# A hybrid decoder trunk on one core: the first projection in another order, index scores and two blocks' search rounds two units earlier

## What is computed

```python
h = rmsnorm(x, norm_mix[l])
proj = h @ w_in[l]
(u, dq, dk, dv, iq, ik, iw, rq, rk, rv, rg) = jnp.split(proj, split_pts, axis=-1)
y_a = s5_mixer(u, ...)                       # state space model on u, 256 wide
y_b = dsa_attention(dq, dk, dv, iq, ik, iw, rel_bias)
y_c = retention(rq, rk, rv, rg, ret_gn[l])
x = x + jnp.concatenate([y_a, y_b, y_c], -1) @ w_out[l]
x = x + swiglu(rmsnorm(x, norm_ffn[l]))

# inside dsa_attention, for a block of 128 queries
dots  = einsum('bqhd,bsd->bqhs', iq, ik)                       # 4 index heads
score = einsum('bqhs,bqh->bqs', relu(dots), iw)
_, sel = top_k(where(causal, score, NEG_INF), 256)             # 256 keys are kept
# softmax attention (8 heads, one shared key and value head) over the kept keys
```

## Time and profile before

| | us |
|---|---|
| median of 3 runs | 2590.75 |
| lowest, highest | 2588.12, 2592.52 |
| the profiled execution | 2596.5 |
| its span, first to last instruction | 2594.7 |
| TensorE busy | 2515.0 (97%) |
| VectorE, ScalarE, GpSimd busy | 1370.1 (53%), 1136.5 (44%), 1319.2 (51%) |
| mean granted clock of TensorE | 0.988 |

### The profile page before, as it was taken

One profiled execution on the slowest core, in us unless ns is written; L12 is line 12 of the kernel. 1 busy time (PEld: TensorE's weight loads), 2 busy tenths in 40 slices (PEclk: granted clock), 3 DMA queues, 4 the chain that ended last, 5 costly groups with the idle time before them and its releaser, 6 DMA issues.

```text
span 2594.7 us, 34756 instructions
## 1 busy us (share of the span) xinstructions
PE 2515.0 (97%) x13515; PEld 1997.8 (77%) x13515; DVE 1370.1 (53%) x2559; ACT 1136.5 (44%) x1726; POOL 1319.2 (51%) x818
## 2 busy tenths in 40 slices
PE   8998979999999999999999999999999999999998
PEld 6777657778777877788777887777887788888887
DVE  3788766987852226842421395589786322211112
ACT  5242355676545433324344422466755453322222
POOL 3432245464645654545555632554655457565654
PEclk9998999999999999999999999999999999999999
DMA  6241112232222353223322342222222225233332
GB/s 169 83 150 42 50 50 90 61 94 74 76 69 66 99 163 98 81 82 90 90 76 81 88 135 58 81 66 82 78 78 63 68 66 203 77 107 101 102 117 89
DMA packets 385666, 232.92 MB, mean 90 GB/s; under 512 B 29592, under 2 KB 371552, under 8 KB 383072
## 3 DMA queue, kind: packets, MB, share of 16 engines
q1 hardware_dynamic: 385136, 229.62, 29.8%
q10 hardware_dynamic: 368, 1.08, 0.1%
HBM read 213.88 MB, written 14.69 MB: 88 GB/s over the span
## 4 chain that ended last, share of the span: by engine, by line
PE 83%; DVE 12%; ACT 2%; issue 2%; DMA 0%; POOL 0%; DVEq 0%; ACTq 0%; SPq 0%
PE psum L1873 79%; PE psum L2203 2%; DVE scores L1431 2%; DVE top L1429 2%; DVE scores L1413 1%; DVE search_i L1453 1%; DVE xs L1245 0%; PE psum L2232 0%; ACT xs L1118 0%; PE psum L2028 0%; DVE scratch L1538 0%; DVE h_lo L1310 0%; PE psum L2307 0%; DVE tmp L1306 0%; ACT xs L1100 0%
## 5 line engine op out<-in xcount | busy, mean ns | idle before, releaser
L769 POOL TENSOR_TENSOR w_lo<-w_raw,w_hi 128x1024 fp32r<-128x1024 f32 (+2 forms) x408 | 902.8, 2213 | 1132.5 <-ACT w_hi L883 1132.4
L1873 PE MATMUL psum<-h_hi,w_hi 128*128 128x512 f32 x1984 | 796.7, 402 | 21.3 <-DVE tmp L1385 8.2
L883 ACT ACTIVATE w_hi<-w_raw 128x1024 fp32r<-128x1024 f32 (+2 forms) x408 | 397.5, 974 | 899.5 <-PE psum L1873 855.6
L1873 PE MATMUL psum<-h_lo,w_hi 128*128 128x512 f32 x1984 | 765.3, 393 | 0.9 <-POOL h_lo L777 0.9
L1873 PE MATMUL psum<-h_hi,w_lo 128*128 128x512 f32 x1984 | 515.7, 391 | 0.0
L1873 PEld LDWEIGHTS psum<-h_hi,w_hi 128*128 128x128 f32 x1984 | 375.4, 189 | 134.7 <-issue 43.9
L1873 PEld LDWEIGHTS psum<-h_lo,w_hi 128*128 128x128 f32 x1984 | 375.0, 189 | 79.0 <-issue 2.2
L1873 PEld LDWEIGHTS psum<-h_hi,w_lo 128*128 128x128 f32 x1984 | 374.1, 189 | 76.9
L1245 DVE TENSOR_TENSOR xs<-xs,psum 128x512 f32<-128x512 f32 x160 | 110.0, 688 | 330.5 <-PE psum L1873 319.6
L1873 PE MATMUL psum<-a_hi,w_hi 128*128 128x512 f32 x704 | 279.3, 397 | 1.1 <-DVE xs L1245 1.1
L1873 PE MATMUL psum<-a_lo,w_hi 128*128 128x512 f32 x704 | 274.6, 390 | 0.0
(11 more groups left out here) (333 smaller groups left out, 3066.1 us busy)
## 6 DMA issues: line engine op xcount, KB each, us to landing
w_raw<-in_w_ffn_in_dram SPq DMA_DIRECT2D x176, 512.0 KB, 3.8
w_raw<-in_w_ffn_out_dram SPq DMA_DIRECT2D x96, 384.0 KB, 3.1
w_raw<-in_w_in_dram SPq DMA_DIRECT2D x68, 512.0 KB, 3.8
w_raw<-in_w_out_dram SPq DMA_DIRECT2D x32, 512.0 KB, 3.6
x_half<-xs SPq DMA_DIRECT2D x8, 1024.0 KB, 6.1
xs<-x_half SPq DMA_DIRECT2D x8, 1024.0 KB, 6.8
w_raw<-in_w_ffn_out_dram SPq DMA_DIRECT2D x32, 256.0 KB, 2.7
out_dram<-mixed SPq DMA_DIRECT2D x8, 512.0 KB, 4.3
```

The costliest lines, as they stand in the source:

```text
L769: eng.tensor_tensor(w_lo(u, n), w_raw[:, u % 3, 0:n], w_hi[:, u % 2, 0:n].bitcast(F32), ALU.subtract).then_inc(sems["weights_ready"], 1)
L883: act(w_hi[:, u % 2, 0:n], w_raw[:, u % 3, 0:n], ACTF.Copy).then_inc(sems["hi_ready"], 1)
L1873: return eng.matmul(out_, lhsT, rhs, start=start, stop=stop, skip_group_check=True)
```

## The change

The first projection of layer 0, half 0, makes its first six units in another order: values and keys, the index key, the two index queries, and then the two S5 inputs. `made` gives the content of a place, `unit_at` the place of a content; the other three projections are as they were. The weight loads, the evictions, the doubling transfers of `kT` and `ikT`, the transposes of `gate` and the waits for `iqT` follow.

With that, steps move. The first `scores` step stands behind unit 4 (it stood behind unit 6), the last behind unit 8 (10). Of the S5 parameters, step 2 stays behind unit 6, step 3 moves from unit 10 to 7 and step 4 from unit 11 to 9. Block 2's 16 rounds all lie in the first projection (10 did). In the second projection block 3's rounds start behind unit 1 of it (unit 4), and 17 of them (12) are in front of the attention steps, which are blended with the 15 (20) that are left.

```diff
+INDEX_FIRST = (U_VK, U_II, U_IQ, U_IQ + 1, 0, 1)
+def made(l, h, i):
+    return INDEX_FIRST[i] if (l, h) == (0, 0) and i < U_RET else i
+def unit_at(l, h, j):
+    return INDEX_FIRST.index(j) if (l, h) == (0, 0) and j < U_RET else j
...
-    out += weave(main[:4], blend(param_steps(0), side)) + main[4:5] + [("rstd", "boot"), ("diag",)]
-    out += place(main[5:15], setup[:2], [sc[0], setup[2]], sc[1:2], sc[2:3], sc[3:4] + rounds(2, 0, 2),
-                 sc[4:] + setup[3:4], setup[4:], rounds(2, 2, 4), rounds(2, 4, 6), rounds(2, 6, 10))
+    out += weave(main[:4], blend(param_steps(0), side)) + main[4:5] + [("rstd", "boot"), ("diag",)] + sc[:1]
+    out += place(main[5:15], sc[1:2] + setup[:2], sc[2:3] + setup[2:3], sc[3:4] + setup[3:4], sc[4:],
+                 rounds(2, 0, 2) + setup[4:], [], rounds(2, 2, 5), rounds(2, 5, 8), rounds(2, 8, 12), rounds(2, 12))
...
-    two = rounds(2, 10)
-    out += place(main[:14], ret[3:5] + prep[:1], ret[5:7] + prep[1:2] + two[:1], ret[7:9] + prep[2:3] + two[1:3],
-                 ret[9:11] + prep[3:4] + two[3:],
-                 ret[11:12] + s5[:1] + three[:2], s5[1:2] + ret[12:13] + three[2:4], ret[13:] + s5[2:3] + three[4:5],
+    out += place(main[:14], ret[3:5] + prep[:1], ret[5:7] + prep[1:2] + three[:1], ret[7:9] + prep[2:3] + three[1:3],
+                 ret[9:11] + prep[3:4] + three[3:5],
+                 ret[11:12] + s5[:1] + three[5:7], s5[1:2] + ret[12:13] + three[7:9], ret[13:] + s5[2:3] + three[9:10],
...
-    side = blend(att[0] + att[1] + att[2], three[12:]) + att[3] + [("attend_end", 0, 0, s) for s in range(2)]
+    side = blend(att[0] + att[1] + att[2], three[17:]) + att[3] + [("attend_end", 0, 0, s) for s in range(2)]
...
-                if i == U_II + 2:
+                if i == unit_at(l, h, U_II) + 2:
...
-                    eng.wait_ge(sems["proj_out"], out_at[U_IQ + 1, h])
+                    eng.wait_ge(sems["proj_out"], out_at[unit_at(l, h, U_IQ + 1), h])
```

More of the change, by code:

```diff
@@ L206, in plan @@
     three = rounds(3)
-    two = rounds(2, 10)
-    out += place(main[:14], ret[3:5] + prep[:1], ret[5:7] + prep[1:2] + two[:1], ret[7:9] + prep[2:3] + two[1:3],
-                 ret[9:11] + prep[3:4] + two[3:],
-                 ret[11:12] + s5[:1] + three[:2], s5[1:2] + ret[12:13] + three[2:4], ret[13:] + s5[2:3] + three[4:5],
-                 s5[3:4] + prep[4:5] + three[5:6], s5[4:6] + prep[5:], s5[6:7] + three[6:8], s5[7:9] + three[8:9],
-                 s5[9:11], s5[11:13] + three[9:10], s5[13:14] + three[10:12])
+    out += place(main[:14], ret[3:5] + prep[:1], ret[5:7] + prep[1:2] + three[:1], ret[7:9] + prep[2:3] + three[1:3],
+                 ret[9:11] + prep[3:4] + three[3:5],
+                 ret[11:12] + s5[:1] + three[5:7], s5[1:2] + ret[12:13] + three[7:9], ret[13:] + s5[2:3] + three[9:10],
+                 s5[3:4] + prep[4:5] + three[10:11], s5[4:6] + prep[5:], s5[6:7] + three[11:13],
+                 s5[7:9] + three[13:14], s5[9:11], s5[11:13] + three[14:15], s5[13:14] + three[15:17])
     att = [attend_steps(0, 0, b) for b in range(TT)]
-    side = blend(att[0] + att[1] + att[2], three[12:]) + att[3] + [("attend_end", 0, 0, s) for s in range(2)]
+    side = blend(att[0] + att[1] + att[2], three[17:]) + att[3] + [("attend_end", 0, 0, s) for s in range(2)]
     out += place(main[14:], *[s5[14:] + side[:2], side[2:8], side[8:14], side[14:21], side[21:]])
@@ L323, in unit_pieces @@
 def unit_pieces(u):
-    kind, _, _, i = UNIT[u]
-    return 2 if kind == "proj" and i == U_VK else 1
+    kind, l, h, i = UNIT[u]
+    return 2 if kind == "proj" and made(l, h, i) == U_VK else 1
 LOADED = []
@@ L594, in load @@
                 kind, l, h, i = UNIT[u]
+                if kind == "proj":
+                    i = made(l, h, i)
                 if u >= 3:
@@ L681, in _ @@
                     kind, l, h, i, u = step
-                    if kind == "proj" and i in (U_VK + 2, U_II + 2):
+                    if kind == "proj" and i - 2 in (unit_at(l, h, U_VK), unit_at(l, h, U_II)):
                         cols = slice(h * HALF, (h + 1) * HALF)
                         n = 2 * l + h
-                        if i == U_VK + 2:
+                        if i - 2 == unit_at(l, h, U_VK):
                             eng.wait_ge(sems["k_out"], n + 1)
@@ L920, in evict_proj @@
                 g = unit_bank("proj", j)
+                j = made(l, h, j)
                 cols = slice(h * HALF, (h + 1) * HALF)
@@ L1957, in proj @@
                 out_at[i, h] = st.now("proj_out")
-                if i == U_II + 1:
-                    eng.wait_ge(sems["proj_out"], out_at[U_II, h])
+                if i == unit_at(l, h, U_II) + 1:
+                    eng.wait_ge(sems["proj_out"], out_at[i - 1, h])
                     take("E")
```

## The result

The changed kernel came out slower. Beside runs of the kernel before on the same chip the ratio of times is 1.0027, with a 95% interval of 1.0014 to 1.0040; of 2590.75 us that is +7.0 us (+3.6 to +10.4). The medians stand further apart (2602.09 us, 2598.27 to 2602.49 in five runs, against 2590.75), which puts the plain median 2.1 us past the end of the predicted range, while the forecast of +4.4 us (a ratio of 1.0017) lies inside the interval of the ratio. Run again later beside the experiments, the same kernel gave 1.0010 (1.0002 to 1.0019), +2.6 us. So it is slower, by an amount about the border of 0.2% that the prediction had drawn.

A forecast was written before the change was run, and what follows sets the result against it. TensorE, busy 97%, bounds the kernel; its early waits come from VectorE's queue. 0 + 7.0 + 2.2 - 0.7 - 4.0 - 0.5 + 0.4 = +4.4 on 2590.75 us, so 2595.2; eight in ten from 2587.5 to 2600.0.

The forecast's parts named there:

- values and keys first: First six units in another order: smaller wait behind `iqT` goes, bank A's copy met bare for 0.78 us; sum 0.
- stall at bank B: Near 91 us TensorE waits for VectorE's copy of bank B, queued behind S5's parameters: +7.0 us, bounds 0 and +8.8.
- slow clock behind it: After the wait at bank B TensorE works 3 to 6 us at about half clock: +2.2 us.
- bank B at unit 15: VectorE's copy of bank B at unit 15 is in time, so its wait goes: -0.7 us.
- rotation's wait and its slow clock: At retention's rotation TensorE's wait of 2.6 us goes, and 1.4 us of slow clock with it.
- from the rotation to S5: Up to the group norm, six rounds of 384 columns (7.9 us) give way to five of 512 (7.4): -0.5 us.
- attention, with what lies between S5's step and it: Attention steps: five rounds fewer give 0.2 us, a wider copy costs 0.6 more; +0.4 us, bounds -0.5 and +1.5.
- bound for both tiles: Upper bound at bank B if two GpSimd tiles lock VectorE out in `s5_set` 4: 99.2 us, +8.8.
- Rival A: Slower, 20%: the rotation is late again, TensorE waits there too and loses the clock again; +8.2 us, 2599.0.
- Rival C: No change, 10%: VectorE's lead at 115 us reaches the waits of 2.7 and 4.0 us, giving bank B's loss back; 2590.8.
- Rival B: Faster, 12%: VectorE reaches the copies in time, needing three lock-outs of 2.2 us less; -5.0 us, 2585.8.
- argument on which waits open and close: In attention, waits for the exponentials cancel; a wait for a 256-column copy replaces one for 128: 0.6 us more.

The follow-up runs named there:

- kernel with small tiles: Changed kernel with GpSimd making only 8 of 1024 columns of `w_lo` for units 9 to 12, low part left out of the products; 0.9990 of the kernel before.
- copies first: Changed kernel with step 4 of the S5 parameters one unit later, behind VectorE's copies of banks B and F; 1.0000 of the kernel before.

## Why the prediction was right, and where it was not

In the order of its steps, predicted against read from the two traces (differences of like rows, after less before):

| step | predicted | read |
|---|---|---|
| up to bank A, without the two waits of the next row | 0 | -0.5 |
| values and keys first (0.78 for bank A, less 0.73 for `iqT`) | 0 | +0.05 |
| stall at bank B | +7.0 | +6.66 |
| slow clock behind it | +2.2 | +2.1 |
| bank B at unit 15 | -0.7 | -0.74 |
| rotation's wait and its slow clock | -4.0 | -4.0 |
| from the rotation to S5 | -0.5 | +3.0 |
| attention, with what lies between S5's step and it | +0.4 | -1.6 |
| all that follows | 0 | +1.0 |
| sum | +4.4 | +5.6 |

(The rows read add up to 6.0. The 0.4 too many lie between unit 14 and the rotation, which TensorE crosses in 17.35 us, where the kernel before takes 17.80 without its waits; the traces do not say why.)

**Right: the copy behind the parameters.** Size, place, cause and consequence held, and the experiments show each: taking `s5_set` 4 from in front of the copies removes the stall, taking 2.5 us of rounds away shortens it by 2.26, taking the tiles away leaves 0.57. VectorE was expected at the copies at 97.4 and came at 96.86. Inside that number two errors cancel. The sum put a lock-out into `s5_set` 2 (4.3 us, as in the earlier trace rows) and one into `s5_set` 4; in fact step 2 ran free and VectorE was done with the two rounds at 84.5 instead of 87.0, and then both tiles of 84.27 and 90.68 fell on step 4, 12.3 us instead of 10.4. The step that copied a window's length from the old order was the weak one: a lock-out belongs to the tile, so it has to be placed anew when steps move. The argument that the second tile of `s5_set` 4 would not be asked for while TensorE stands was wrong, too: it came at 90.68, ahead of the stall. And the bound for both tiles was added up 0.4 us short: 87.0 + 12.6 is 99.6, so +9.2 and not +8.8, and 2.2 us above the sum and not 1.8.

**Right at its place: the rotation.** Two lock-outs fell on it (3.30 and 3.42 us), VectorE was done at 138.17 and TensorE started at 138.29, with 0.1 us in hand where the prediction had seen 0.3. Rival A, the late rotation, missed by that. What the sum did not have is that the clock then fell at the next wait (below).

**Right: it is not nothing.** Rival C rested on what VectorE has in hand at 115 us reaching the later waits. It did not: VectorE still waited 5.34 us for TensorE until 166.72, and the waits at the group norm and at S5 were 2.37 and 6.89 us for 2.70 and 4.02. With the same 13515 matmuls, and VectorE at 52 to 54% in every kernel, the order of the steps moved the time from 1.0027 to 0.9940. Rival B needed three lock-outs less; the kernel with small tiles had just that and came out at 0.9990, 2.6 us under the kernel before, where B had 5.

**Wrong: from the rotation to S5, -0.5.** The prediction compared rounds (7.4 us for 7.9) and took the rest as it was. It read +3.0: 0.56 of wait put down to issue and 0.24 more at retention, 1.5 for a clock that fell at 155 us, 0.9 for a new wait at 176, and 0.2 less later. The 0.9 is again a lock-out: under a tile VectorE's L1712 took 2.86 us for 0.68, where in the kernel before the tile had fallen on L1705 (2.16 us for 0.62), and a round of 512 columns stands behind it in place of one of 384. The 0.56 put down to issue stands in every trace in which TensorE does not wait for the rotation (0.52 to 0.58), and in none of the five in which it does. The 1.5 us for the clock are a term that the prediction did not have. From retention's wait to the next one (151.30 to 162.07 in the kernel before) the rows are, for the kernel before and the changed one:

```profile
151.30:162.07 10.77, 9.86 (x89) 1.00 1.04 371
155.27:167.53 12.26, 11.35 (x88) 0.86 0.88 311
```

In all 11 traces in which the rotation's transposes ran at full clock, the clock fell here and cost 1.4 to 2.8 us, with a wait at the rotation ("copies first") or without. Of the three in which it had fallen at the rotation, it fell here in one. So the 1.4 us that the sum booked as regained at the rotation were lost again 15 us later. Whether the one fall stands in for the other, or the new order of the first projection brings it about, the runs do not show. S5's wait grew from 4.0 to 6.9 us while the slow clock in front of it vanished, and that costs nothing more: the changed kernel is 6.14 us later at 204.81, ahead of it, and 6.16 us later at 216.09, behind it.

**Wrong in size and sign: attention, +0.4.** That the rounds hide there was right (13.6 us of waits in both orders, and alone). The argument on which waits open and close came to zero in the sum, not to 0.6. The 1.5 us that were gained were one fall of the clock that did not happen. The +1.0 after attention is put down to the clock as well, since no step of the change reaches there; that is argued and not shown.

So the direction and the likeliest cause were right, and the total was right partly by luck, because the two largest misses, +3.5 and -2.0, have opposite signs. The chances, 0.52 for "same" and 0.41 for slower, are not settled by the runs: the interval of the first measurement lies mostly above the border, that of the second below it. One reading was too broad: later on TensorE is not busy 99% everywhere, but 94.5 to 97% in six of the stretches of 100 us up to 2000; nothing in the sum rests on it.

## What to carry to other kernels

Before work moves up in an engine's list, look for what in that list another engine will ask for soon, here the copy that frees a bank: fill VectorE's gaps behind such an operation, never ahead of it. Cost the list anew at the new place, tile by tile of the engine that locks it out, here GpSimd, since a lock-out stays with the tile and not with the step. And when a wait is removed, look up the next place of the same kind in the next stage at once: with the copies and the rotation cleared the time was 0.9984, with most of the waits for the group norm and S5 gone as well 0.9975, and with the rest of S5's and 1.3 us of retention's gone 0.9940.

## What the runs showed of the hardware that I had not expected

- The waits repeat and the clock does not. In the four traces with the full stall it was 6.66, 6.65, 6.65 and 6.65 us, and what the clock cost behind it was 2.1, 1.9, 2.6 and 2.2 (computed as above). Two executions of one program differed by 8.3 us of TensorE's busy time.
- A shorter wait does not cost less clock: 2.97 us behind a wait of 4.39, 2.14 behind one of 6.66. And waits of like length at one place can cost it or not: at the rotation 1.4 us behind 2.59, nothing behind 2.87.
- A lock-out costs about the rest of the tile whatever the size of the VectorE operation: 0.16 became 2.0 to 2.4, 0.68 became 2.86, 1.23 became 3.3 to 3.4 us.
